# An encoder block with a mixture of experts on one core: the last expert's pass by halves of its inner columns, and a final stage by halves without GpSimd

## What is computed

```python
def run_block(args):                       # one expert, 128 gathered rows
    xb, e = args
    gu = xb @ w_gate_up[e] + b_gate_up[e]  # 1024 -> 2 x 1024
    return clamped_swiglu(gu) @ w_down[e] + b_down[e]

ys = ys.astype(jnp.float32) * row_gate[:, None]
out = jax.ops.segment_sum(ys, row_tok, num_segments=T + 1)[:T]
x = x + moe(h2, ...)
return rmsnorm(x, g_final)
```

## Time and profile before

| | us |
|---|---|
| median of 3 runs (lowest to highest) | 1514.19 (1513.93 to 1515.33) |
| the profiled execution | 1513.34 |
| its span (first to last instruction) | 1511.6 |

### The profile page before, as it was taken

How to read it: one execution, slowest core, us unless ns; L and a number is a source line. 1 busy time by engine, 2 the same in 40 slices (tenths; PEclk the granted TensorE clock), 3 DMA queues, 4 the chain that set the end, 5 groups by cost and what they waited for, 6 DMA issues and landing times.

```text
span 1511.6 us, 21699 instructions
## 1 busy us (share of the span) xinstructions
PE 1491.3 (99%) x7207; PEld 1228.9 (81%) x7207; DVE 1350.5 (89%) x1055; ACT 1151.5 (76%) x1258; POOL 448.4 (30%) x215
## 2 busy tenths in 40 slices
PE   8999999999999999999999999999999999999997
PEld 6888789886788888888888888888888888888884
DVE  5477587656999999999999999999999999999985
ACT  6355588235888888888888888888888888888873
POOL 1002245401342313243223323233423233233321
PEclk9999999998999999999999999999999999999999
DMA  7330001535999999999999999999999999999973
GB/s 260 112 112 28 1 1 57 212 140 179 395 362 388 378 381 383 382 379 375 382 359 396 370 387 379 381 369 380 381 368 382 369 390 367 389 373 386 380 261 125
DMA packets 130514, 457.17 MB, mean 302 GB/s; under 512 B 13970, under 2 KB 14490, under 8 KB 130484
## 3 DMA queue, kind: packets, MB, share of 16 engines
q1 hardware_dynamic: 118708, 435.19, 75.6%
q0 software_dynamic: 9360, 16.51, 4.3%
q10 hardware_dynamic: 2416, 5.07, 0.9%
HBM read 451.77 MB, written 22.54 MB: 314 GB/s over the span
## 4 chain that ended last, share of the span: by engine, by line
PE 96%; DVE 2%; ACT 1%; DMA 0%; issue 0%; ACTq 0%; SPq 0%; DVEq 0%
PE ps L1568 28%; PE ps L1570 28%; PE ps L1569 28%; PE ps L1857 2%; PE ps L1865 2%; PE ps L1626 1%; PE ps L1669 1%; PE ps L1670 1%; PE ps L1799 0%; PE ps L1611 0%; DMA raw<-in_w_in 0%; ACT probs L821 0%; PE ps L1643 0%; PE ps L1644 0%; PE ps L1647 0%; PE ps L1649 0%
## 5 line engine op out<-in xcount | busy, mean ns | idle before, releaser
L1403 DVE TENSOR_TENSOR chunk_lo<-chunk,chunk_hi 128x2048 fp32r<-128x2048 f32 x384 | 902.4, 2395 | 5.3 <-ACT chunk_hi L935 3.7
L935 ACT ACTIVATE chunk_hi<-chunk 128x2048 fp32r<-128x2048 f32 x378 | 719.4, 1912 | 71.7 <-PE ps L1570 71.7
L1568 PE MATMUL ps<-chunk_hi,XT 128*128 128x512 f32 x1024 | 404.4, 395 | 0.3 <-DVE XT L1443 0.3
L1570 PE MATMUL ps<-chunk_hi,XT 128*128 128x512 f32 x1024 | 399.1, 390 | 0.0
L1569 PE MATMUL ps<-chunk_lo,XT 128*128 128x512 f32 x1024 | 398.9, 390 | 0.0
L679 POOL DMA_INDIRECT sum_rows<-y,idx x31 | 129.9, 4190 | 443.6 <-ACT y L1084 417.4
L1570 PEld LDWEIGHTS ps<-chunk_hi,XT 128*128 128x128 f32 x1024 | 192.2, 188 | 40.3
L1568 PEld LDWEIGHTS ps<-chunk_hi,XT 128*128 128x128 f32 x1024 | 192.4, 188 | 39.1 <-DVE XT L1443 0.8
L1569 PEld LDWEIGHTS ps<-chunk_lo,XT 128*128 128x128 f32 x1024 | 192.5, 188 | 38.1
L1568 PE MATMUL ps<-chunk_hi,hidT 128*128 128x512 f32 x512 | 199.3, 389 | 0.5 <-DVE hidT L1450 0.5
L1570 PE MATMUL ps<-chunk_hi,hidT 128*128 128x512 f32 x512 | 199.2, 389 | 0.0
(11 more groups left out here) (282 smaller groups left out, 2025.9 us busy)
## 6 DMA issues: line engine op xcount, KB each, us to landing
chunk<-in_w_gate_up SPq DMA_DIRECT2D x256, 1024.0 KB, 11.2
chunk<-in_w_down SPq DMA_DIRECT2D x128, 1024.0 KB, 9.7
raw<-in_w_in SPq DMA_DIRECT2D x14, 1024.0 KB, 5.4
xs<-in_x SPq DMA_DIRECT2D x8, 512.0 KB, 6.5
w_out<-in_w_out SPq DMA_DIRECT2D x4, 1024.0 KB, 6.0
raw<-in_w_branch_a SPq DMA_DIRECT2D x2, 1024.0 KB, 5.4
raw<-in_w_branch_b SPq DMA_DIRECT2D x2, 1024.0 KB, 6.3
sum_rows<-xs ACTq DMA_DIRECT2D x4, 512.0 KB, 2.7
```

Source lines behind the costliest of these rows:

```text
L935: a.activation(chunk_hi[hi_slot(c, nxt)][:, :], chunk[c][:, :], ACT.Copy).then_inc(ex_hi, 1)
L1403: v.tensor_tensor(chunk_lo[c][:, :], chunk[c][:, :], chunk_hi[hi_slot(c, nxt, first)][:, :].bitcast(F32), ALU.subtract).then_inc(ex_lo, 1)
L1568: mm(dst, lhsT(0), rhs(0), start=start, stop=False, skip_group_check=seeded)
L1570: return mm(dst, lhsT(1), rhs(0), start=False, stop=stop, skip_group_check=seeded)
```

## The change

The last item gets functions of its own on the three engines (`act_last`, `dve_last`, `pe_last`), and the branch `nxt` disappears from the loop's, which stay the same otherwise.

- TensorE: the up product runs over all four chunks for the first 512 of its output columns (`up_half` tells VectorE), then the place transposes, then over the chunks again for the second 512; between chunks 5 and 7 of that second sweep, and between down products 8 and 9, four transposes each of the hidden rows (`half_T`). `ex_used` is raised in the second sweep.
- VectorE and ScalarE make the hidden rows and their parts by halves (`half_hid`, `half_lo`, `half_hi`); ScalarE splits chunk 9 ahead of its copy of the place table.
- The unread matmuls go; all four blocks' bias products stand behind the down products, each block's right ahead of its sum products, and for the last block (2) half by half.
- Block 0 is scaled by VectorE as the others are; GpSimd has nothing of the final stage. Stores are issued in the order of `ENDS`.
- The last block is summed, squared, scaled and stored in halves of 512 columns; the first half's sum of squares goes through an added Identity on ScalarE (x 1/D + eps) and enters the root of the second as its bias.

```diff
+            def act_last(i):
+                rows_out(i - 1, 12 * i + 6)
+                ex_split_hi(i, 8, False)
+                ex_split_hi(i, 9, False)
+                act.wait_ge(placeT_ps, 1)
+                a.activation(placeT[:, :, :], ps[0:CAP, 6, :].rearrange("p (c n) -> p c n", n=128),
+                             ACT.Copy).then_inc(placeT_out, 1)
+                ex_split_hi(i, 10, False)
+                half_hi(i, 0)
+                ex_split_hi(i, 11, False)
+                half_hi(i, 1)
+            c = ENDS[-1]
+            act.wait_ge(sums_ready, NT)
+            a.activation(fin_sq[:, c, 0:512], fin[:, c, 0:512], ACT.Square, accum_out=cmax[:, 0:1]).then_inc(fsq_done, 1)
+            act.wait_ge(fsq_done, NT)
+            a.activation(npass[:, 0:1], cmax[:, 0:1], ACT.Identity, bias=eps[:, 0:1], scale=1.0 / D)
+            act.wait_ge(sums_ready, NT + 1)
+            a.activation(fin_sq[:, c, 512:D], fin[:, c, 512:D], ACT.Square,
+                         accum_out=ss[:, c:c + 1]).then_inc(fsq_done, 1)
+            act.wait_ge(fsq_done, NT + 1)
+            a.activation(ss[:, c:c + 1], ss[:, c:c + 1], ACT.Sqrt, bias=npass[:, 0:1],
+                         scale=1.0 / D).then_inc(frt_done, 1)
...
+            def dve_last(i):
...
+                ex_split_lo(i, 8, False)
+                dve.wait_ge(up_half, 1)
+                half_hid(i, 0)
+                ex_split_lo(i, 9, False)
+                half_lo(i, 0)
+                dve.wait_ge(ex_used, 12 * i + 10)
+                half_hid(i, 1)
+                ex_split_lo(i, 10, False)
+                half_lo(i, 1)
+                ex_split_lo(i, 11, False)
...
-                if n:
-                    dve.wait_ge(inv_ready, n + 1)
-                    v.scalar_tensor_tensor(out=fin[:, c, :], in0=fin[:, c, :], scalar=rstd[:, c:c + 1], in1=gfin,
-                                           op0=ALU.mult, op1=ALU.mult).then_inc(out_dve, 1)
+                dve.wait_ge(inv_ready, n + 1)
+                for cols in (slice(0, D),) if n < NT - 1 else (slice(0, 512), slice(512, D)):
+                    v.scalar_tensor_tensor(out=fin[:, c, cols], in0=fin[:, c, cols], scalar=rstd[:, c:c + 1],
+                                           in1=gfin[:, cols], op0=ALU.mult, op1=ALU.mult).then_inc(out_dve, 1)
...
-            add_up(3)
+            add_half(0)
+            add_half(1)
             finish(2)
             finish(3)
...
+            def pe_last(i):
...
+                pe.wait_ge(up_seeded, i + 1)
+                for t in range(2):
+                    for c in range(4, 8):
+                        if t == 0:
+                            pe.wait_ge(ex_lo, order(i, c, False) + 1)
+                        for k in range(2):
+                            last = mm_split(ps[0:CAP, 2 + t, :], lambda p: XT[:, p, 2 * (c - 4) + k, :],
+                                            lambda p: expert_w(c, hi_slot(c, False), p, k, t), start=False,
+                                            stop=(c == 7 and k == 1), seeded=True)
+                        if t:
+                            last.then_inc(ex_used, 1)
+                        if (t, c) == (1, 5):
+                            pe.wait_ge(placeT_out, 1)
+                            half_T(i, 0)
+                    if t == 0:
+                        last.then_inc(up_half, 1)
+                        pe.wait_ge(place_ready, 1)
+                        for c in range(NT):
+                            last = t_.transpose(ps[0:CAP, 6, c * 128:(c + 1) * 128], place[:, c, :], ident[:, :])
+                        last.then_inc(placeT_ps, 1)
+                        pe.wait_ge(gathered, (i + 2) * 16)
+                        pe.sem_inc(xt_ps, 1)
+                pe.wait_ge(y_ready, i + 1)
+                pe.wait_ge(hidT_lo, i + 1)
+                product(8, hidT, 4, True, False)
+                half_T(i, 1)
+                product(9, hidT, 4, False, False)
+                pe.wait_ge(hidT_lo, i + 2)
+                product(10, hidT, 4, False, False)
+                product(11, hidT, 4, False, True)
...
+                for t in range(2):
+                    mm(ps[:, 2 * c + t, :], gateT[:, c * 128:(c + 1) * 128], bd[:, t * 512:(t + 1) * 512],
+                       start=True, stop=False)
+                    if n == NT - 1:
+                        place_sum(c, t)
+                if n < NT - 1:
+                    for t in range(2):
+                        place_sum(c, t)
```

More of the change, by code:

```diff
@@ L499, in _ @@
                 sp.dma_start(fin[:, c, :], acc_v[c]).then_inc(acc_in[c], 16)
-            for n in (1, 0, 2, 3):
-                c = ENDS[n]
-                if n:
[L503 to L507, removed]
+            for n in range(NT - 1):
+                sp.wait_ge(out_dve, n + 1)
+                sp.dma_start(out_v[ENDS[n]], fin[:, ENDS[n], :]).then_inc(out_stored, 16)
+            for t in range(2):
+                half = slice(t * 512, (t + 1) * 512)
+                sp.wait_ge(out_dve, NT + t)
+                sp.dma_start(out_v[ENDS[-1]][:, half], fin[:, ENDS[-1], half]).then_inc(out_stored, 16)
+            sp.wait_ge(out_stored, 16 * NT + 16)
         @block.gpsimd
@@ L1092, in act_item @@
+            def act_item(i, before=True):
+                ex_split_hi(i + 1, 0)
+                ex_split_hi(i + 1, 1)
                 if before:
                     rows_out(i - 1, 12 * i + 6)
[L1094 to L1103, removed]
@@ L1127, in _ @@
+                ex_split_hi(i, 11)
+                if not isinstance(i, int):
+                    act.wait_ge(scattered, 16 * i)
+                index_rows(i + 3, bass.ds((i + 3) % 4, 1))
+                a.activation(warm[:, :], eps[:, :], ACT.Sigmoid)
+                ex_split_hi(i + 1, 4)
+                ex_split_hi(i + 1, 5)
+                sigmoid(12 * i + 14)
+                ex_split_hi(i + 1, 6)
+                ex_split_hi(i + 1, 7)
+            act_item(0, False)
             with act.Fori(1, last_item) as i:
[L1128 removed]
@@ L1485, in _, with half_hid @@
             glu(1)
[L1487 to L1502, removed]
+            def half_hid(i, t):
+                cols = slice(t * 512, (t + 1) * 512)
+                v.tensor_scalar(hid[:, cols], ps[0:CAP, 2 + t, :], 8.0, -6.0, ALU.min, ALU.max).then_inc(clip_ready, 1)
+                dve.wait_ge(clip_ready, i + 1 + t)
+                dve.wait_ge(glu_ready, i + 1)
+                v.scalar_tensor_tensor(out=hid[:, cols], in0=sg[:, cols], scalar=SILU_TOP, in1=hid[:, cols],
+                                       op0=ALU.min, op1=ALU.mult).then_inc(hid_ready, 1)
@@ L1503, in dve_item @@
+            def dve_item(i):
+                dve.wait_ge(idx_done, i + 3)
+                serve(i + 3)
+                for c in range(3):
+                    ex_split_lo(i + 1, c)
+                rows_lo(i + 2, 0)
+                ex_split_lo(i + 1, 3)
                 dve.wait_ge(ex_used, 12 * i + 10)
@@ L1968, in pe_item, with half_T, product @@
                 product(11, hidT, 4, False, True)
+            def half_T(i, t):
+                pe.wait_ge(hid_ready, i + 1 + t)
+                for k in range(4):
+                    last = t_.transpose(ps[:, 6 + t, k * CAP:(k + 1) * CAP],
+                                        hid[:, t * 512 + k * 128:t * 512 + (k + 1) * 128], ident[0:CAP, 0:CAP])
+                last.then_inc(hidT_ps, 1)
+            def pe_last(i):
+                def product(c, src, bank, start, stop):
+                    weigh(order(i, c, False), c, hi_slot(c, False), src, bank, start, stop).then_inc(ex_used, 1)
+                pe.wait_ge(up_seeded, i + 1)
[12 more added lines that the diff above has]
+                            half_T(i, 0)
+                    if t == 0:
+                        last.then_inc(up_half, 1)
[5 more added lines that the diff above has]
+                        pe.sem_inc(xt_ps, 1)
+                pe.wait_ge(y_ready, i + 1)
+                pe.wait_ge(hidT_lo, i + 1)
[5 more added lines that the diff above has]
+                product(11, hidT, 4, False, True)
```

165 lines of the change are left out of this document (69 added, 96 removed).

## The result

The changed kernel takes 1520.64 us (median of 6 runs, 1517.11 to 1522.93), the kernel before 1513.97 in the same comparison (6 runs, 1513.04 to 1515.33): a ratio of 1.004, with a 95% interval of 1.003 to 1.005. It is 6.7 us slower where I forecast 3.7 faster, and outside the range of 1509.1 to 1512.7.

A forecast was written before the change was run, and what follows sets the result against it. TensorE, busy 99% of the span, was taken to bound the kernel, so only the end could move. Terms 1.1 + 0.65 + 1.4 + 0.3 + 0.3 (stores) = 3.7 us took the median from 1514.19 to 1510.5; range 1509.1 to 1512.7.

The forecast's parts named there:

- part 3: Final stage: VectorE scales block 0 without GpSimd, last block goes by halves; last store issued 3.44 us earlier, at 1504.98.
- My 0.04 for slower: Behind the down products TensorE's clock falls to 1.2 GHz; kernel could end at about 1522.9 us; chance 0.04.
- Part 1, the pass by halves: Last expert's pass sorted by output halves: TensorE reaches the end of the down products 5.5 us earlier.
- The rival that the pass waits: Last pass waits 0.7 to 2 us, leaving 1.7 to 3.0 of gain, around 1511.8; chance 0.27.
- Part 2, the biases: All bias products in the tail: 4.4 of 5.5 us are given back, TensorE is done 1.1 earlier.
- 1.1 (TensorE): End of the kernel: TensorE's last matmul ends at 1501.1 instead of 1502.23, a gain of 1.1 us.
- 0.65: Last block's sum on VectorE started 0.65 us after its matmuls could release it; that lateness goes.
- 1.4 (no contention): Scaling of block 3 on VectorE takes 1.28 us instead of 2.66 without GpSimd's multiply beside it.
- 0.3: Last block's sum, square and scaling by halves, less the added small operations, gain 0.3 us.
- My walk of VectorE's queue: Final stage's sums, reciprocals and scalings followed in order on VectorE; last store issued at 1504.98, against 1508.42.
- Part 4: Last block's store in halves gains 0.3 us beyond the earlier issue; bounds nothing and 0.65.
- The Identity loaded no table: Rival: Identity between Square and Sqrt on ScalarE costs two table loads of 1.28 us, giving 1513.1; chance 0.04.

## Why the prediction was wrong

**The step that failed** is the removal of GpSimd's final operations, in part 3 ("That is the second gain: without GpSimd it is 1.28") and in the list of rivals. I priced what those operations cost while they run, and what VectorE takes over, and asked of GpSimd's queue only what waits behind. I didn't ask in which state they leave the engine, and none of my rivals touched the start of the launch. My 0.04 for slower was for the clock behind the down products; the granted clock there is 1.00 (2.4 GHz) from 1499 to 1513, and the mechanism was another. The runs showed in its place a wait of 11.2 us in front of the next launch's first affine select, against 0.49 before, while the end gained the 3.8 that I had summed up. What can be said for the prediction is that the price stood in no row of before: there the swap at line 515 costs 0.49 us of idle with its wait, and the swap at 699 is hidden in a wait of 28.8. But the condition stood there. Lines 699 and 701 are the only general operations of GpSimd behind the expert loop's broadcasts, and the trace has a load for line 699, at 1474.2.

**Part 1, the pass by halves: right.** 5.5 us earlier was forecast, and it is 5.52 (28.83 to 23.31). No wait in the pass: VectorE's subtractions for the two halves of the hidden rows start 9.92 and 15.84 us after the up product's start, my walk had 10.0 and 15.8. The rival that the pass waits did not come true. (The 2.85 for 12 matmuls behind a transpose is not half of 5.57 but what 2.72 leaves of it; 1471.21 to 1474.06 bears it out.)

**Part 2, the biases: right.** The last sum matmul is at 35.52, where 35.3 was forecast. The 0.2 lies in the last block's two half pairs of bias products: from the start of each to its first sum matmul there are 1.05 us, where I had half of a pair, 0.96.

**Part 3: right in its total, wrong in its terms.** I wrote 1.1 (TensorE) + 0.65 + 1.4 (no contention) + 0.3. As separate terms the runs refute these. TensorE's last matmul comes 0.9 earlier. Without GpSimd the old order gains nothing (43.03 against 43.01), since VectorE, which has hardly any idle time there, takes on 1.3 for the 1.4; in the new order GpSimd's absence is worth 0.5 at the last issue and 0.8 at the end. The new final stage on the old pass gains 0.2 to 0.4 at the end, and nothing before the last issue, with the clock's loss taken off. With the pass it is 3.78. What joins them is VectorE's work: four sums, four reciprocals and four scalings, some 10 us. In the old order they start when block 0's sum is ready, 32.08 us after the last up product's start, all four are ready within 5 us, and VectorE ends last. In the new one block 0's sum is ready at 26.56, the bias pairs between the sums space them by 3.0, and VectorE works in those gaps. TensorE keeps 0.9 of the 5.5 us, VectorE has all 5.5 of them. My walk of VectorE's queue had this (last issue forecast at 39.6, measured 39.58), so the total is no luck; my list of terms hid it, and that is why the forecast for the old pass with the new final stage missed, by 1.9 in time and 2.4 at the last issue.

**Part 4: right within what the traces can tell.** 0.1 to 0.24 for the store by halves (0.3 forecast). The Identity loaded no table: it stands at 1512.58 with 0.29 in the timeline above, and the square follows it.

With one column's multiply at GpSimd's end the forecast is met: 1509.81 against 1510.5, by ratio 0.9968 against the 0.9976 forecast. That kernel is faster than both.

**What stays open.** Whether the swap at the start depends on the same program having run just before was not tried with two programs in turn. The runs show that the last kind of operation decides; that what it leaves behind is loaded code rests on the instruction's name and on the Trainium skill, "GPSIMD Engine Reference", section 2.1. Nor is it shown how much of the 7.6 us at the start and the 5.9 at the end comes from their being two different codes. The dip of the clock behind the old pass's hole came in two profiled executions of four; I can't say what decides.

## What to carry to other kernels

Before an instruction is removed, ask which state it leaves in its engine, and who starts from that state; the next launch of the same kernel is one of those who do. Where a profile's first microseconds change although the code there didn't, look at the end of the launch. In this kernel GpSimd should end a launch on the kind of operation with which the launch begins; an operation of one column does it, since it has some 13 us of idle time to hide in. And when an edit moves work for one engine, walk the queue of the engine behind it as a whole: gains that depend on one queue don't add up.

## What the runs showed of the hardware that I had not expected

- The code that GpSimd was left with outlives a launch. Swapping it at the start of a launch held the affine select back by 10.9 to 11.5 us beside SP's loads, in four kernels that left the broadcast's code, by 7.6 in a fifth that held the loads back, and by 0.49 with its wait in the seven that left the general code.
- Bringing in the broadcast's code took 5.9 us at the end of a launch with the DMA engines idle. Bringing in the general code took 7.6 at the start with them idle. In the five profiled kernels with the multiply and no broadcast behind it, the general code took 10.1 to 11.1 us from the load's issue to the multiply, beside the last weight loads.
- Behind the hole of the old pass (bias products, unread matmuls and transposes for 6 us) the granted clock fell in two of four profiled executions, at 1.6 us each. The new pass has no hole, and its last down matmul starts 22.99 us after its first up matmul in all of the eight profiled executions that have it.
